# Handing the last quarter of the residual additions to GpSimd, and ordering ScalarE's high parts before its squares

## The reference

```
def rms_norm_2(x, g):
    x32 = x.astype(jnp.float32)
    y = x32 * lax.rsqrt(jnp.mean(x32 * x32, axis=-1, keepdims=True) + EPS)
    return (y * g.astype(jnp.float32)).astype(x.dtype)

for l in range(DEPTH):                       # DEPTH = 2
    h = rms_norm_2(x, norm_mix_pre[l])
    ...                                      # four branches -> merged
    x = x + rms_norm_2(merged @ w_out[l], norm_mix_post[l])
    h2 = rms_norm_2(x, norm_ffn_pre[l])
    gu = h2 @ w_ffn_in[l]
    f_g, f_u = jnp.split(gu, 2, axis=-1)
    f = (jax.nn.silu(f_g) * f_u) @ w_ffn_out[l]
    x = x + rms_norm_2(f, norm_ffn_post[l])
```

## Time and profile before

| | us |
|---|---|
| median of 3 runs | 2258.08 (2256.72 to 2259.97) |
| the profiled execution's own time | 2255.04 |
| its span, first to last instruction | 2253.2 |
| TensorE busy | 2110.4 (94%) |
| VectorE busy | 1514.5 (67%) |
| ScalarE busy | 1150.2 (51%) |
| GpSimd busy | 561.5 (25%) |
| mean granted TensorE clock | 0.972 of full speed |

### The profile page before, as it was taken

How to read it: one execution, slowest core, us unless ns; L and a number is a source line. 1 busy time by engine, 2 the same in 40 slices (tenths; PEclk the granted TensorE clock), 3 DMA queues, 4 the chain that set the end, 5 groups by cost and what they waited for, 6 DMA issues and landing times.

```text
span 2253.2 us, 43766 instructions
## 1 busy us (share of the span) xinstructions
PE 2110.4 (94%) x18160; PEld 1970.9 (87%) x18160; DVE 1514.5 (67%) x2244; ACT 1150.2 (51%) x1919; POOL 561.5 (25%) x668
## 2 busy tenths in 40 slices
PE   6999989999999999899999989989997989999997
PEld 5986679999999886689988889989996889998997
DVE  3657766777777666668776769755556677865554
ACT  4535545555655643555556555554444655554443
POOL 0012321332333002213321144104330134212331
PEclk9999999999999998999999999999998999999999
DMA  8546544555555454345544335535552434453552
GB/s 345 178 143 230 206 169 147 191 188 171 168 196 184 140 163 159 129 143 192 191 159 155 131 118 183 179 121 197 188 188 105 158 114 150 144 196 133 190 191 85
DMA packets 103205, 378.37 MB, mean 168 GB/s; under 512 B 11456, under 2 KB 11744, under 8 KB 101984
## 3 DMA queue, kind: packets, MB, share of 16 engines
q1 hardware_dynamic: 101520, 367.31, 47.6%
q10 hardware_dynamic: 1488, 8.27, 1.0%
HBM read 374.49 MB, written 1.05 MB: 167 GB/s over the span
## 4 chain that ended last, share of the span: by engine, by line
PE 33%; issue 13%; POOL 5%; DVE 3%; ACT 3%; POOLq 0%; DVEq 0%; ACTq 0%
PE ps L406 10%; PE ps L408 10%; PE ps L407 10%; POOL R L2596 2%; POOL R L2638 1%; DVE WL L1637 1%; PE ps L481 1%; POOL R L2441 1%; PE ps L420 1%; POOL X L2399 1%; PE ps L421 1%; ACT WH L1005 1%; PE ps L428 1%; DVE RST L1673 1%; DVE TMP L1647 0%
## 5 line engine op out<-in xcount | busy, mean ns | idle before, releaser
L406 PE MATMUL ps<-X,WH 128*128 128x256 f32 x4384 | 1242.6, 283 | 15.3 <-DVE WL L1637 7.9
L407 PE MATMUL ps<-X,WH 128*128 128x256 f32 x4384 | 1228.4, 280 | 0.0
L408 PE MATMUL ps<-X,WL 128*128 128x256 f32 x4384 | 1227.4, 280 | 0.0
L1637 DVE TENSOR_TENSOR WL<-RAW,WH 128x1024 fp32r<-128x1024 f32 (+2 forms) x608 | 773.6, 1290 | 452.9 <-ACT WH L1005 451.1
L406 PEld LDWEIGHTS ps<-X,WH 128*128 128x128 f32 x4384 | 827.0, 189 | 30.0 <-DVE WL L1637 11.7
L407 PEld LDWEIGHTS ps<-X,WH 128*128 128x128 f32 x4384 | 826.9, 189 | 1.7
L408 PEld LDWEIGHTS ps<-X,WL 128*128 128x128 f32 x4384 | 826.9, 189 | 0.0
L1005 ACT ACTIVATE WH<-RAW 128x1024 fp32r<-128x1024 f32 (+2 forms) x608 | 623.8, 1045 | 263.6 <-PE ps L408 261.5
L2441 POOL TENSOR_SCALAR R<-CONS,SM 128x128 f32<-128x128 f32 x128 | 83.8, 666 | 319.6 <-DVE SM L1832 308.9
L2535 POOL TENSOR_TENSOR TMP<-TMP 128x256 f32<-128x256 f32 x66 | 48.9, 741 | 446.6 <-ACT TMP L1354 443.1
L1155 ACT ACTIVATE PB<-ps,SM 128x512 f32<-128x512 f32 (+1 forms) x152 | 87.6, 583 | 140.9 <-DVE SM L1822 140.5
(11 more groups left out here) (194 smaller groups left out, 2204.0 us busy)
## 6 DMA issues: line engine op xcount, KB each, us to landing
RAW<-w_dram SPq DMA_DIRECT2D x674, 512.0 KB, 3.7
RAW<-w_dram SPq DMA_DIRECT2D x16, 480.0 KB, 3.2
BIG<-big_dram ACTq DMA_DIRECT2D x4, 1024.0 KB, 5.2
RAW<-w_dram SPq DMA_DIRECT2D x8, 320.0 KB, 2.7
RAW<-w_dram SPq DMA_DIRECT2D x6, 384.0 KB, 2.9
XT<-x_dram ACTq DMA_DIRECT2D x2, 1024.0 KB, 7.5
CONS<-con_dram ACTq DMA_DIRECT2D x1, 1169.0 KB, 9.7
out_dram<-XT SPq DMA_DIRECT2D x1, 1024.0 KB, 3.9
```

The source lines that it names most:

```text
L406: e.matmul(out, a.hi, b.hi, start=start and i == 0, stop=False, skip_group_check=open_bank)
L407: e.matmul(out, a.hi, b.lo, start=False, stop=False, skip_group_check=open_bank)
L408: last = e.matmul(out, a.lo, b.hi, start=False, stop=stop and i == n - 1, skip_group_check=open_bank)
L1637: e.tensor_tensor(weights(i).lo, raw(i), weights(i).hi.bitcast(F32), ALU.subtract).then_inc(*w_lo.mark(i))
```

## The change

At each of the four places GpSimd now scales and adds the last pair (chunks 6 and 7) of `Y8` and `X2`, by the same two operations on the same 128 x 512 tiles; VectorE keeps the pairs 0 to 2 (`staged(3, ...)`). GpSimd waits for the same reciprocal as VectorE, and between its two operations for its own result. Readers of the last pair wait for GpSimd's mark `merged(tag, "x")`: `added` chooses the mark by the pair. The output's transfer waits for both engines, and the row `k.rst[0]` is given free by both.

At the mixer norm ScalarE makes all eight high parts first and then the eight squares, where it went pair by pair.

```diff
+        def added(tag, n):
+
+            return resid(tag, n) if n < 3 else merged(tag, "x")
...
-            q.wait_ge(*resid("end", 3))
+            q.wait_ge(*resid("end", 2))
+            q.wait_ge(*merged("end", "x"))
             e.dma_start(out_d, X2).then_inc(s_out, 16)
...
                 def post_add(tag, nxt):
-                    k.rst[0].free = [scaled(tag, "s", 3)]
+                    k.rst[0].free = [scaled(tag, "s", 2), pooled(tag, "s")]
                     for n in range(4):
                         if nxt is not None:
-                            nxt.add(X2[:, 2 * n], resid(tag, n))
+                            nxt.add(X2[:, 2 * n], added(tag, n))
                             nxt.add(X2[:, 2 * n + 1])
...
                 for n in range(4):
-                    q.wait_ge(*resid(("post", l), n))
+                    q.wait_ge(*added(("post", l), n))
                     for c in (2 * n, 2 * n + 1):
                         e.activation(H.hi[:, c], X2[:, c], ACT.Copy, scale=par("fpre", l)[:, c:c + 1]).then_inc(*x_hi.mark(("fpre", l), c))
-                    for c in (2 * n, 2 * n + 1):
-                        ss.add(X2[:, c])
+                for c in range(8):
+                    ss.add(X2[:, c])
...
-                    for _ in staged(4, scale_two, add_two):
+                    for _ in staged(3, scale_two, add_two):
                         pass
...
+                def post_add(tag, ready, y_ready):
+                    q.wait_ge(*ready)
+                    q.wait_ge(*y_ready)
+                    e.tensor_tensor(Y8[:, 6:8], Y8[:, 6:8], k.rst[0].ap.unsqueeze(1).to_broadcast([128, 2, 256]), ALU.mult).then_inc(*pooled.mark(tag, "s"))
+                    q.wait_ge(*pooled(tag, "s"))
+                    e.tensor_tensor(X2[:, 6:8], X2[:, 6:8], Y8[:, 6:8], ALU.add).then_inc(*merged.mark(tag, "x"))
+
+                post_add(("post", l), recips(("post", l)), copied("post", l, 7))
...
                 feed_forward(silu_gate, first=scale_gate)
+                post_add(("fpost", l) if l + 1 < DEPTH else "end", recips(("fpost", l)), scaled("y", l, 7))
```

More of the change, by code:

```diff
@@ L1597, in post_add @@
                 def post_add(tag, nxt):
-                    k.rst[0].free = [scaled(tag, "s", 3)]
+                    k.rst[0].free = [scaled(tag, "s", 2), pooled(tag, "s")]
                     for n in range(4):
                         if nxt is not None:
-                            nxt.add(X2[:, 2 * n], resid(tag, n))
+                            nxt.add(X2[:, 2 * n], added(tag, n))
                             nxt.add(X2[:, 2 * n + 1])
-                k.rst[0].free = [scaled(("post", l), "s", 3)]
+                k.rst[0].free = [scaled(("post", l), "s", 2), pooled(("post", l), "s")]
                 ss = SquareSum(("fpre", l), 8, k.sq2[0])
                 for n in range(4):
-                    q.wait_ge(*resid(("post", l), n))
+                    q.wait_ge(*added(("post", l), n))
                     for c in (2 * n, 2 * n + 1):
                         e.activation(H.hi[:, c], X2[:, c], ACT.Copy, scale=par("fpre", l)[:, c:c + 1]).then_inc(*x_hi.mark(("fpre", l), c))
-                    for c in (2 * n, 2 * n + 1):
-                        ss.add(X2[:, c])
+                for c in range(8):
+                    ss.add(X2[:, c])
                 ss.rstd(1024, k.rst[1])
```

## The result

In the timing beside each other the kernel before took 2256.42 us (19 runs, 2251.96 to 2260.47) and the changed kernel 2261.86 us (19 runs, 2256.36 to 2266.60): 5.4 us more by the medians; the ratio is 1.0023 with a 95% interval of 1.0015 to 1.0032 (+5.2 us, +3.4 to +7.2). A second timing, among the experiments, gave 1.0013 (1.0001 to 1.0024).

A forecast was written before the change was run, and what follows sets the result against it. TensorE, busy 94% of the span, was taken as the bound, so only its stalls or slow stretches pay. End 0.9, feed-forward norm 2.1 and mixer norms 0.8 sum to +3.8 us on 2258.1: 2261.9, range 2257.5 to 2266.0.

The forecast's parts named there:

- two larger terms: Feed-forward norm of layer one +2.1 us and end of the program +0.9 us.
- The price of a turn: Shared port of VectorE and GpSimd: each GpSimd operation holds VectorE up by 1.05 us, 2.1 together.
- rival of the long hold: All four places: GpSimd's broadcast scaling holds the port twice as long; total +6.9 us, 2265.0; chance 0.12.
- VectorE keeps the port: All four places: VectorE runs its six operations first, GpSimd works afterwards; total +1.5 us, 2259.6; chance 0.07.
- no contention: All four places: the engines don't hold each other up; total -5.2 us, 2252.9; chance 0.08.
- End, +0.9: End of the program: VectorE's last addition ends 0.9 us later and nothing hides it.
- Feed-forward norm, +2.1: Layer one: squares hang on add 1, so +2.1 us; the two operations saved on VectorE bring nothing.
- Mixer norms, +0.4 each: Two mixer norms: chunk 6 starts at 1512.0 instead of 1511.17, clock rise as before; +0.4 us each, 0.8 both.
- The first rival: Mixer norms: clock rises 4.8 us after TensorE's restart, -0.3 and -0.8 us; total +1.9, 2260.0; chance 0.20.
- it turns 2.1 into 0.66: Mixer norms: ScalarE's order saves 3 x 0.61 us before chunk 6, cutting the delay from 2.1 to 0.66 us.
- old stall of 0.17: Mixer norm: TensorE's 0.17 us stall inside the old chunk 6, forecast to be gone, leaving a 0.66 us delay.
- What would show it: Signs in the changed profile, among them VectorE's first addition starting 3.3 us behind the reciprocal instead of 1.25.

The follow-up runs named there:

- one turn: Changed kernel with GpSimd's scaling of the last pair left out, its addition kept; stages 15.31, 12.37, 16.52, 9.09 us, no whole time given.
- writing alone: Changed kernel with GpSimd's two operations replaced by writes of zeros that read nothing; stages 14.94, 11.29, 14.61, 8.02 us, no whole time given.
- the pair left out: Changed kernel with the last pair neither scaled nor added on any engine; 2250.69 us, ratio 0.9981 to the kernel before.
- second trace of before: The kernel before, unchanged, profiled a second time; stages 16.80, 11.29, 16.78, 9.22 us.
- the move alone: Changed kernel with ScalarE back to pair by pair, GpSimd keeping the last pair; 2265.39 us, ratio 1.0043 to the kernel before.
- kernel before kept busy: Kernel before plus ten spare TensorE products in the idle time ahead of the feed-forward part at both mixer norms; ratio 0.9983 to the kernel before.
- order kept busy: Kernel before with ScalarE's new order and ten spare TensorE products ahead of the feed-forward part; ratio 0.9972 to the kernel before.

## Why the prediction was right, and where it was off

The forecast was +3.8 us, 2261.9; measured were +5.2 (3.4 to 7.2) and, the second time, +2.9 (0.2 to 5.4). Both intervals hold +3.8. The mechanism and the two larger terms (3.0 of the 3.8) came out as forecast. That the total fits as well is in part luck: the 0.8 of the mixer norms is not seen in the stages, and the first timing lies above their sum. Whether the change passes 0.2% is not settled by them: the first lies just beyond it, the second below.

- **The price of a turn.** Forecast 1.05 us for each GpSimd operation, measured 1.07 and 1.05; the order of turns is as forecast, and the experiments with one turn, none and writing alone show the cause. The broadcast operand, whose bound was twice that, costs nothing extra: the rival of the long hold falls. So does "VectorE keeps the port" (it would have left add 0 on time) and "no contention" (it would have looked like the pair left out).
- **End, +0.9.** Measured 10.16 - 9.23 = +0.93.
- **Feed-forward norm, +2.1.** Measured 13.42 - 11.29 = +2.13, in every execution with the move; and that the two operations saved bring nothing there is shown by the pair left out.
- **Mixer norms, +0.4 each.** About right in the delay, not borne out in the price. Chunk 6 was forecast 0.83 us later (1512.0 instead of 1511.17) and is 0.97 later in both traces of the changed kernel. The price rested on a rise of the clock at the same moment as in one trace of before, 11.0 us behind the reciprocal. In the four passages with the change it rose 7.9, 8.2, 10.3 and 10.6 us behind it, and in the second trace of before 10.5 and 10.4. Against the mean of before (17.0) the four passages were -1.0, -0.8, +0.2 and +0.3, on average -0.35 where +0.4 was forecast. The first rival (an earlier rise) came true in one execution of two, at -1.0 and -1.3 against the trace of before instead of the -0.3 and -0.8 that its 4.8 us gave: the rise came 3.1 and 3.5 us behind the restart. It deserved more than its 0.20.
- **ScalarE's order, "it turns 2.1 into 0.66".** Right in kind, a little small: 0.97 less the old stall of 0.17 is 0.80. Its worth was left implicit: alone it gives -4.7 us. It brings chunk 6 forward by 0.81 us, and with it the clock rose sooner. In the four passages with the order and without GpSimd's work the rise came 4.7 to 5.9 us behind TensorE's restart (two traces), in the four of before 7.8 to 9.4; that the closed gaps are the reason is likely and not shown. The move takes most of the gain at the mixer norms away again and adds 3.06 us at the other two places.
- **What would show it.** One sign was put wrongly: the first addition was to *start* 3.3 us behind the reciprocal. It starts 2.32 us behind and ends 2.1 us later than before, because the profile counts the time before the port as part of the operation.

Left open: the stages of the whole change add up to +3.06 at the two narrow places and about -0.35 at each mixer norm, +2.4, and the two timings average about +4; for the move alone they are +5.3 and +9.7. From the first reciprocal to the end the traces give +1.6 for the whole change (means of two) and +6.2 for the move alone, close to the stages, so the traces show no other place that pays. The timed intervals are some 4 to 7 us wide, and the kernel before kept busy was timed 3.8 us less with no stage to show for it: a gap of this size between timing and stages stays unexplained.

## What to carry to other kernels

An operation handed from VectorE to GpSimd is not free when both engines read two tiles from SBUF at that moment. Inside a burst on the critical path each GpSimd operation held VectorE up by 1.05 us here, to save it 0.60. Ask first which operation of the burst the next engine waits for. At the feed-forward norm these were the first two additions, and taking work off the tail bought nothing even when GpSimd did none of it; at the end of the program, where the last addition counts, it would have bought 1.2 us (8.03 instead of 9.23) against a price of 2.1. Reordering the reader (all high parts ahead of all squares) gained 4.7 us, and the move gained nothing at any place. Two edits in one change should be timed apart: here one hid the other.

## What the runs showed of the hardware

- The two engines went in turns at the port, one operation each: VectorE's further ready operations never got in front of a waiting operation of GpSimd (scale 1 and add 0 both end late, 2.36 instead of 1.29 us and 1.74 instead of 0.69). The Trainium skill ("SBUF — State Buffer", section "Who interferes with whom") says that the later one stands still until the other has finished and that a GpSimd operation that only writes doesn't contend with a VectorE operation with two SBUF inputs. The traces agree with both: 2.36 instead of 1.29 us in the first case, 1.29 in the second.
- The wait before the port is hidden inside the durations, on both engines. A duration above that of the undisturbed operation (1.76 against 1.28 us on GpSimd, 1.74 against 0.69 on VectorE) is the only sign of it in these traces.
- The clock fell in the middle of a pass although spare work had kept TensorE at 2.4 GHz until the pass began: with gaps of 0.5 us and TensorE busy for 1.04 us of two (kernel before kept busy), and with gaps of 0.3 us at the second mixer norm of the order kept busy. At the first mixer norm of that same execution, with the same gaps, it stayed up. So the length of the gaps does not settle it; filling the idle time ahead of a pass kept the clock through it in three of six passages.

The stretch of the first mixer norm of the order kept busy, in which the clock stayed up:

```profile
1512.00:1514.00 2.00, 1.56 (x8) 1.15 (x8) 2.00 (x5) 1.71 (x6) 0.00 (x0) 1.00 0.00 0
```
